# Recurrent layer: the head gates of steps 0 to 4 as three products of high and low parts, with low parts made on GpSimd

## The chip, the cores and the metric

The kernel runs on one core of a Trainium2 chip. The number that counts is the device time of one execution in microseconds, as the median of several executions. The chip's compute engines work side by side, each in its own program order, and wait for one another by semaphores: PE (TensorE, matrix products), DVE (VectorE), ACT (ScalarE), POOL (GpSimd) and SP (which here only starts transfers).

## The reference

A network of four layers on 256 positions of 1024 channels, in fp32: gated linear attention with a convolutional feed-forward part, softmax attention with another, then a recurrent layer ("LRU") and a short-convolution layer. Only the recurrent layer is touched:

```
u = h @ w_in;  gate, xb = split(u)                      # 1536 channels each
xc = causal_depthwise_conv(xb, conv_w, conv_b)          # 4 taps
g = sigmoid(einsum('bshi,hio->bsho', xc in 12 heads, gate_w) + gate_b)   # 12 heads of 128 -> 256
r, i = split(g);  log_a = -8 * r * softplus(-lambda)
h_t = exp(log_a) * h_{t-1} + sqrt(-expm1(2 log_a)) * i * xc
out = (h * silu(gate)) @ w_out
```

The head gates are the einsum: one 128x256 weight block for each of the 12 heads.

## The kernel before

All weights of the large products arrive by a stream of 1 MB units. Each unit is taken apart into two fp32r tensors (a 32-bit type whose products cost PE less than fp32 ones): ACT copies it to `w_hi` (L511) and DVE subtracts that from the raw unit to give `w_lo` (L1004). With activations in high and low parts too, a product is then three fp32r products, high x high, high x low and low x high (`PARTS`). The head gates are the exception in this layer: `gatew`, all 12 heads, is loaded whole by four transfers from POOL's queue (L492), and the gates multiply it with `xc` in plain fp32 (L2243).

The recurrent layer runs in six steps of two heads (`LRU_ITERS`), j = 0 to 5, written out on every engine as a loop in Python, so that the order on each engine is the order of the code. In step j:

- PE does `wide` for the unit "x" of step j (48 products, L1847, into one PSUM bank), `gates(j-1)`, `wide` for the unit "g" of step j (48 more, which waits for `gate_free` j), and from step 2 `lru_down(j-2)`, 24 products of 512 columns (L1862) that wait for `a_lo` of that step. In step 5, `gates(5)` stands between "g" and `lru_down(3)`.
- ACT takes the branch out of PSUM (`branch_taken`, xb), then the tanhs of `gates(j-1)` (L832: rg, ig) and `tanhs` (L854: ug), starts the convolution (`lru_taps`, L864: xc), and does `decays`, `roots` (L878, which wait for POOL's `clamped`), weight copies (L511), `gated` (L890) and `act_high` (L896: a_hi, which waits for DVE's `act_ready`).
- DVE does `inputs_gated(j-1)` (L1542: iu from ig and xc), six instructions of `lru_conv(j)` (L1555), after whose last `conv_ready` is raised, `recurrence(j-1)` (L1573, L1581, two scans L1566, L1587), weight subtractions (L1004), `lru_gate(j)` (L1601, which raises `gate_free`) and `act_low` (L1607: a_lo).
- POOL has one instruction in a step: it clamps ug at zero (L496).

`lru_taps` of step j waits for `inputs_gated(j-1)`, since that still reads the old xc; the convolution waits for the taps; and `gates(j)` on PE waits for the convolution.

## Time and profile before

| | us |
|---|---|
| median of 3 runs | 858.86 (858.73 to 859.99) |
| the profiled execution | 860.18 |
| its span, first to last instruction | 858.3 |
| busy PE | 847.7 |
| busy DVE | 677.3 |
| busy ACT | 542.2 |
| busy POOL | 38.3 |

The mean granted clock of TensorE is 0.999 of full speed. The busy times are sums over the whole program; the recurrent layer takes the stretch from about 570 to 680 us. One step of it from step 2 on takes 18.7 us.

### The profile page before, as it was taken

The numbers are of one execution on the slowest core, as the hardware profiler recorded it, in microseconds if no ns is written. First come the engines' busy times: TensorE is split into PE (matmuls) and PEld (weight loads), VectorE is DVE, ScalarE is ACT, GpSimd is POOL, SyncE is SP. The second block draws the span as 40 slices with busy tenths as digits, with TensorE's granted clock in tenths as the row PEclk, the third lists the DMA queues.
The fourth block names the chain that finished last, engine by engine and source line by source line (L and its number), as shares of the span: only waits on it lengthen the run. The fifth ranks groups of instructions, "written<-read, shape, count | busy, mean of one in ns | idle before, by whom it ended". The sixth has DMA issues, their size and how long they took to land.

```text
span 858.3 us, 13362 instructions
## 1 busy us (share of the span) xinstructions
PE 847.7 (99%) x4881; PEld 746.4 (87%) x4881; DVE 677.3 (79%) x970; ACT 542.2 (63%) x746; POOL 38.3 (4%) x57
## 2 busy tenths in 40 slices
PE   8999999999999999999999999999999999999997
PEld 7988889888888888889888888889999898888886
DVE  6799878887878798868887886787987877776764
ACT  5745656657556566576666656578988764555533
POOL 1000100000000041000000000000010100000000
PEclk9999999999999999999999999999999999999999
DMA  7554354666654344224666655435364046545511
GB/s 261 221 191 155 145 195 153 239 229 209 215 211 160 144 183 160 99 99 150 243 218 243 228 201 210 150 133 211 137 239 165 0 149 246 211 178 221 220 50 49
DMA packets 22908, 152.80 MB, mean 178 GB/s; under 512 B 2608, under 2 KB 2736, under 8 KB 5712
## 3 DMA queue, kind: packets, MB, share of 16 engines
q1 hardware_dynamic: 22176, 149.45, 47.5%
q0 software_dynamic: 544, 2.49, 0.9%
q8 instruction: 29, 0.48, 0.2%
q10 hardware_dynamic: 144, 0.26, 0.1%
q14 instruction: 15, 0.12, 0.0%
HBM read 151.14 MB, written 1.05 MB: 177 GB/s over the span
## 4 chain that ended last, share of the span: by engine, by line
PE 97%; DMA 1%; ACT 1%; DVE 1%; SPq 0%; issue 0%; ACTq 0%
PE ring L1798 38%; PE acc L1862 31%; PE ring L1847 10%; PE ring L1809 4%; PE acc L2085 3%; PE ring L1828 2%; PE ring L1933 1%; PE ring L2067 1%; PE ring L2243 1%; PE acc L1756 1%; DMA raw<-in_stream_dram 1%; PE ring L2125 1%; PE ring L2145 0%; PE acc L1882 0%; PE ring L1970 0%; PE ring L2162 0%
## 5 line engine op out<-in xcount | busy, mean ns | idle before, releaser
L1004 DVE TENSOR_TENSOR w_lo<-raw,w_hi 128x2048 fp32r<-128x2048 f32 (+1 forms) x145 | 317.9, 2197 | 5.8 <-ACT w_hi L511 5.7
L511 ACT ACTIVATE w_hi<-raw 128x2048 fp32r<-128x2048 f32 (+1 forms) x146 | 266.9, 1840 | 52.4 <-DMA raw<-in_stream_dram 50.0
L1798 PE MATMUL ring<-hh,w_hi 128*128 128x512 f32 x944 | 223.9, 390 | 0.0
L1798 PEld LDWEIGHTS ring<-hh,w_hi 128*128 128x128 f32 x944 | 175.3, 188 | 35.1
L1798 PEld LDWEIGHTS ring<-hh,w_lo 128*128 128x128 f32 x944 | 117.4, 192 | 2.5
L1798 PE MATMUL ring<-hh,w_lo 128*128 128x256 f32 x944 | 118.3, 283 | 0.0
L1862 PE MATMUL acc<-w_hi,a_hi 128*128 128x512 f32 x264 | 103.6, 392 | 0.1
L1862 PE MATMUL acc<-w_lo,a_hi 128*128 128x512 f32 x264 | 102.9, 390 | 0.0
L1862 PE MATMUL acc<-w_hi,a_lo 128*128 128x512 f32 x264 | 102.8, 389 | 0.0
L1847 PE MATMUL ring<-hh,w_hi 128*128 128x256 f32 x480 | 87.8, 285 | 0.0
L1122 DVE TENSOR_TENSOR usum<-ring,usum 128x512 f32<-128x512 f32 x65 | 44.7, 688 | 54.2 <-ACT usum L516 54.2
L1330 DVE SCALAR_TENSOR_TENSOR cacc<-usum,par,cacc 128x255 f32<-128x255 f32 x168 | 73.8, 481 | 15.0 <-ACT cacc L669 9.8
L1862 PE MATMUL acc<-w_hi,hh 128*128 128x512 f32 x256 | 84.2, 399 | 0.2 <-DVE hh L1043 0.2
L1847 PEld LDWEIGHTS ring<-hh,w_hi 128*128 128x128 f32 x480 | 75.4, 192 | 0.5
L1847 PE MATMUL ring<-hh,w_lo 128*128 128x256 f32 x240 | 67.9, 283 | 0.0
L516 ACT ACTIVATE usum<-ring 128x512 f32<-128x512 f32 x65 | 38.2, 588 | 44.4 <-PE ring L1798 42.6
L1862 PEld LDWEIGHTS acc<-w_hi,a_hi 128*128 128x128 f32 x264 | 49.6, 188 | 11.6 <-issue 0.9
L1862 PEld LDWEIGHTS acc<-w_hi,a_lo 128*128 128x128 f32 x264 | 49.6, 188 | 10.4
L1862 PEld LDWEIGHTS acc<-w_lo,a_hi 128*128 128x128 f32 x264 | 49.6, 188 | 9.8
L1862 PEld LDWEIGHTS acc<-w_hi,hh 128*128 128x128 f32 x256 | 48.1, 188 | 10.5 <-issue 0.4
L1862 PE MATMUL acc<-w_lo,hh 128*128 128x512 f32 x128 | 49.9, 390 | 0.0
L669 ACT ACTIVATE cacc<-usum,par 128x256 f32<-128x256 f32 x84 | 45.5, 590 | 6.9 <-DVE usum L1122 6.9
(247 smaller groups left out, 961.1 us busy)
## 6 DMA issues: line engine op xcount, KB each, us to landing
raw<-in_stream_dram SPq DMA_DIRECT2D x134, 1024.0 KB, 4.8
raw<-in_stream_dram SPq DMA_DIRECT2D x12, 512.0 KB, 3.8
gatew<-in_gatew_dram POOLq DMA_DIRECT2D x4, 384.0 KB, 4.2
x<-in_x_dram SPq DMA_DIRECT2D x2, 512.0 KB, 3.6
out_dram<-xn SPq DMA_DIRECT2D x3, 256.0 KB, 2.6
row<-in_row_dram POOLq DMA_DIRECT2D x1, 640.0 KB, 6.1
gup_raw<-in_gup_dram SPq DMA_DIRECT2D x3, 128.0 KB, 11.6
par<-in_par_dram SPq DMA_DIRECT2D x1, 274.0 KB, 4.8
```

Of the source, the lines that this page charges most:

```text
L511: nc.scalar.activation(w_hi[:, u % RING, 0:n], raw[:, u % RAW, 0:n], ACT.Copy).then_inc(hi_split, 1)
L516: nc.scalar.activation(usum[:, k, :, :], ring[:, 2 * k:2 * k + 2, S:2 * S], ACT.Copy).then_inc(cross_ready, 1)
L669: last = nc.scalar.activation(cacc[:, k, half, :], ring[:, 2, half * S:(half + 1) * S] if alone else usum[:, k, half, :], ACT.Identity, sc ...
L1004: nc.vector.tensor_tensor(w_lo[:, u % RING, 0:n], raw[:, u % RAW, 0:n], w_hi[:, u % RING, 0:n].bitcast(f32), ALU.subtract).then_inc(lo_spl ...
L1122: nc.vector.tensor_tensor(usum[:, k, :, :], ring[:, 2 * k:2 * k + 2, 0:S], usum[:, k, :, :], ALU.add).then_inc(summed, 1)
L1330: last = nc.vector.scalar_tensor_tensor(out=cacc[:, k, half, out_at], in0=at, scalar=par[:, bass.ds(c, 1)], in1=cacc[:, k, half, out_at], ...
L1798: last = nc.tensor.matmul(into, w_parts[part][:, u % RING, lo:lo + P], moving(kc), start=(n, kc) == (0, 0), stop=(n, kc) == (1, KC - 1), s ...
L1809: last = nc.tensor.matmul(both, w_hi[:, (u + k) % RING, lo:lo + P], hh[:, kc, :, t * P:(t + 1) * P], start=first, stop=end, skip_group_che ...
L1828: nc.tensor.matmul(ring[:, 2 * k + f, 0:S], w_lo[:, (u + k) % RING, lo:lo + P], h_hi[:, kc, :], start=False, stop=False, skip_group_check= ...
L1847: last = nc.tensor.matmul(ring[:, b, f * S:(f + 1) * S], w_parts[a][:, slot, lo:lo + P], h_parts[c][:, kc, :], start=kc == 0 and n == 0, s ...
L1862: last = nc.tensor.matmul(acc[:, t, half * 512:(half + 1) * 512], lhs(a, kc, t), w_parts[c][:, slot, j * D + half * 512:j * D + (half + 1) ...
L2085: last = nc.tensor.matmul(acc[:, t, half * 512:(half + 1) * 512], of_h(a, kc, t), w_parts[c][:, (U_AQ + n) % RING, j * D + half * 512:j * ...
```

## The change

For steps 0 to 4 (`SPLIT_GATES`), the head gates use the same three fp32r products as everything else. Of the weights, ACT makes `gw_hi` for the two heads of a step (a copy of 128x512), and POOL makes `gw_lo` by a subtraction, into the place of `gatew`. Of the activations, in step 0 ACT makes `xc_hi` and DVE makes `xc_lo`; in steps 1 to 4 POOL makes both, with a copy and then a subtraction, after `conv_ready`. PE waits for `gw_split` and `xc_split` in place of `conv_ready`. `gates(5)` stays in fp32.

```
+SPLIT_GATES = range(LRU_ITERS - 1)
...
+        gw_hi = put("gw_hi", [P, 2, 2 * P], f32r, at=gup_at)
+        gw_lo = put("gw_lo", [P, LRU_HEADS, 2 * P], f32r, at=gatew_at)
+        xc_lo = put("xc_lo", [P, 2, S], f32r, at=gup_at + 16 * P)
+        xc_hi = put("xc_hi", [P, 2, S], f32r, at=stage_at + 4 * 14 * S)
...
@@ gpsimd
+            def gate_weights_low(e):
+
+                pool.wait_ge(gw_hi_ready, e + 1)
+                nc.gpsimd.tensor_tensor(gw_lo[:, 2 * e:2 * e + 2, :], gatew[:, 2 * e:2 * e + 2, :], gw_hi[:, :, :].bitcast(f32),
+                                        ALU.subtract).then_inc(gw_split, 1)
+
+            gate_weights_low(0)
             for e in range(LRU_ITERS):
                 pool.wait_ge(tanh_ready, 2 * e + 2)
                 nc.gpsimd.tensor_scalar(ug[:, :, :], ug[:, :, :], 0.0, None, ALU.max).then_inc(clamped, 1)
+                if e + 1 in SPLIT_GATES:
+                    gate_weights_low(e + 1)
+                    pool.wait_ge(conv_ready, e + 2)
+                    nc.gpsimd.tensor_copy(xc_hi[:, :, :], xc[:, :, :]).then_inc(xc_hi_ready, 1)
+                    pool.wait_ge(xc_hi_ready, e + 2)
+                    nc.gpsimd.tensor_tensor(xc_lo[:, :, :], xc[:, :, :], xc_hi[:, :, :].bitcast(f32), ALU.subtract).then_inc(xc_split, 1)
@@ scalar
+            def gate_weights_high(e):
+
+                if e == 0:
+                    act.wait_ge(gatew_loaded, 16 * 4)
+                nc.scalar.activation(gw_hi[:, :, :], gatew[:, 2 * e:2 * e + 2, :], ACT.Copy).then_inc(gw_hi_ready, 1)
...
                 if j:
                     gates(e)
                     tanhs(e)
+                    if j in SPLIT_GATES:
+                        gate_weights_high(j)
+                else:
+                    gate_weights_high(0)
                 lru_taps(j)
                 if j < 2:
                     gated(j)
+                if j == 0:
+                    act.wait_ge(conv_ready, 1)
+                    nc.scalar.activation(xc_hi[:, :, :], xc[:, :, :], ACT.Copy).then_inc(xc_hi_ready, 1)
@@ vector
                 if j < 2:
                     lru_gate(j)
+                if j == 0:
+                    dve.wait_ge(xc_hi_ready, 1)
+                    nc.vector.tensor_tensor(xc_lo[:, :, :], xc[:, :, :], xc_hi[:, :, :].bitcast(f32), ALU.subtract).then_inc(xc_split, 1)
@@ tensor, gates(e)
-                pe.wait_ge(conv_ready, e + 1)
+                if e in SPLIT_GATES:
+                    pe.wait_ge(gw_split, e + 1)
+                    pe.wait_ge(xc_split, e + 1)
+                else:
+                    pe.wait_ge(conv_ready, e + 1)
...
-                        last = nc.tensor.matmul(ring[:, HEAD_BANKS[k], r * S:(r + 1) * S],
-                                                gatew[:, 2 * e + k, r * P:(r + 1) * P], xc[:, k, :],
-                                                start=True, stop=True, skip_group_check=True)
+                        into, at = ring[:, HEAD_BANKS[k], r * S:(r + 1) * S], slice(r * P, (r + 1) * P)
+                        if e not in SPLIT_GATES:
+                            last = nc.tensor.matmul(into, gatew[:, 2 * e + k, at], xc[:, k, :], start=True, stop=True, skip_group_check=True)
+                            continue
+                        for n, (a, c) in enumerate(PARTS):
+                            last = nc.tensor.matmul(into, (gw_hi[:, k, at], gw_lo[:, 2 * e + k, at])[a], (xc_hi, xc_lo)[c][:, k, :],
+                                                    start=n == 0, stop=n == 2, skip_group_check=True)
```

How the order of instructions stands on the engines, at three places. Lines are those of each kernel's own file, and the number behind a name is its buffer's. First POOL, from the last statistics of the layer before to those of the next; the kernel before:

```order
L492 DMA gatew_79<-in_gatew_dram 128x768 [waits used] x4
L448 TENSOR_SCALAR half_mean_64<-stat_66 128x1 [waits sumsq] x2
L496 TENSOR_SCALAR ug_120<-ug_120 128x512 [waits tanh_ready] x6
L448 TENSOR_SCALAR half_mean_64<-stat_66 128x1 [waits sumsq] x4
L186 UNCONDITIONAL_BRANCH
```

The changed kernel, for steps 0 to 2:

```order
L506 TENSOR_TENSOR gw_lo_128<-gatew_79,gw_hi_127 128x512 [waits gw_hi_ready]
L512 TENSOR_SCALAR ug_120<-ug_120 128x512 [waits tanh_ready]
L506 TENSOR_TENSOR gw_lo_128<-gatew_79,gw_hi_127 128x512 [waits gw_hi_ready]
L516 CAST xc_hi_130<-xc_117 128x512 [waits conv_ready]
L518 TENSOR_TENSOR xc_lo_129<-xc_117,xc_hi_130 128x512 [waits xc_hi_ready]
L512 TENSOR_SCALAR ug_120<-ug_120 128x512 [waits tanh_ready]
```

Between two clamps now stand three instructions of 128x512, four times over; the six clamps ran one after another with nothing between them.

Next PE at `gates(1)`, between the last products of "x" and the first of "g". Before:

```order
L1847 MATMUL ring<-hh_53,w_lo_51 128x256
L2243 MATMUL ring<-xc_117,gatew_79 128x256 [waits ri_ready,conv_ready]
L2243 MATMUL ring<-xc_117,gatew_79 128x256 x3
L1847 MATMUL ring<-hh_53,w_hi_50 128x256 [waits gate_free,lo_split]
L1847 MATMUL ring<-hh_53,w_hi_50 128x256
```

After, its first product and the start of the second:

```order
L1886 MATMUL ring<-hh_53,w_lo_51 128x256
L2291 MATMUL ring<-xc_hi_130,gw_hi_127 128x256 [waits ri_ready,xc_split,gw_split]
L2291 MATMUL ring<-xc_lo_129,gw_hi_127 128x256
L2291 MATMUL ring<-xc_hi_130,gw_lo_128 128x256
L2291 MATMUL ring<-xc_hi_130,gw_hi_127 128x256
```

Four fp32 products have become four triples, and the wait on the convolution one on the two low parts.

Last ACT, at the end of step 0 and into step 1. Before:

```order
L890 ACTIVATE sgate_124<-gg_122 128x512 [waits gate_summed]
L511 ACTIVATE w_hi_50<-raw_49 128x2048 [waits used,raw_loaded1]
L511 ACTIVATE w_hi_50<-raw_49 128x2048 [waits used,raw_loaded2]
L511 ACTIVATE w_hi_50<-raw_49 128x2048 [waits used,raw_loaded0]
L821 ACTIVATE xb_123<-ring 128x512 [waits conv_ready,used]
```

After:

```order
L919 ACTIVATE sgate_124<-gg_122 128x512 [waits gate_summed]
L942 ACTIVATE xc_hi_130<-xc_117 128x512 [waits conv_ready]
L533 ACTIVATE w_hi_50<-raw_49 128x2048 [waits used,raw_loaded1]
L533 ACTIVATE w_hi_50<-raw_49 128x2048 [waits used,raw_loaded2]
L533 ACTIVATE w_hi_50<-raw_49 128x2048 [waits used,raw_loaded0]
```

The copy of xc stands ahead of the three weight copies, and DVE's subtraction (xc_lo) likewise ahead of its three.

## Rows read from the trace of the kernel before

**Rows 1.** The page: busy us by engine; shares of the chain that ended last.
```profile
PE 847.7 (99%) x4881; PEld 746.4 (87%) x4881; DVE 677.3 (79%) x970; ACT 542.2 (63%) x746; POOL 38.3 (4%) x57
...
PE 97%; DMA 1%; ACT 1%; DVE 1%; SPq 0%; issue 0%; ACTq 0%
```
**Rows 2.** The chain in order of time, recurrent layer: start us, us, what, count.
```profile
601.54 1.73 PE ring L2243 x8
603.27 5.75 PE ring L1847 x48
...
666.98 9.57 PE acc L1862 x42
```
**Rows 3.** PE's timeline: start us, us, instruction, count; gates(1), lru_down(0), gates(2), gates(5).
```profile
601.38 1.89 PE L2243 MATMUL ring<-xc,gatew 128*128 128x256 f32 x8
...
608.86 0.40 PE L1862 MATMUL acc<-w_hi,a_hi 128*128 128x512 f32 x1
...
620.08 1.89 PE L2243 MATMUL ring<-xc,gatew 128*128 128x256 f32 x8
...
664.98 1.99 PE L2243 MATMUL ring<-xc,gatew 128*128 128x256 f32 x8
```
**Rows 4.** ACT's timeline in the recurrent layer: start us, us, instruction, count.
```profile
585.83 5.50 ACT L511 ACTIVATE w_hi<-raw 128x2048 fp32r<-128x2048 f32 x3
...
593.14 1.10 ACT L854 ACTIVATE ug<-rg,sp 128x256 f32<-128x256 f32 x2
...
603.53 0.62 ACT L896 ACTIVATE a_hi<-iu 128x512 fp32r<-128x512 f32 x1
```
**Rows 5.** POOL's timeline over the program; in brackets the idle time before.
```profile
2.01 0.41 POOL L430 TENSOR_SCALAR_AFFINE_SELECT causal<-causal 128x256 f32<-128x256 f32 x1
...
312.45 2.12 POOL L477 TENSOR_TENSOR tabs<-rope,row 128x256 f32<-128x256 f32 x1 [5.06 <-PE acc L1756]
314.54 0.46 POOL L478 TENSOR_TENSOR tabs<-rope,row 128x128 f32<-128x128 f32 x1
...
315.39 0.74 POOL L477 TENSOR_TENSOR tabs<-rope,row 128x256 f32<-128x256 f32 x1
316.10 2.51 POOL L478 TENSOR_TENSOR tabs<-rope,row 128x128 f32<-128x128 f32 x1
...
594.32 1.51 POOL L496 TENSOR_SCALAR ug<-ug 128x512 f32<-128x512 f32 x1 [25.06 <-ACT ug L854]
```
**Rows 6.** DVE's timeline beside POOL's instructions of 312 to 318 us.
```profile
311.68 2.29 DVE L1004 TENSOR_TENSOR w_lo<-raw,w_hi 128x2048 fp32r<-128x2048 f32 x1 [0.73 <-ACT w_hi L511]
...
318.21 2.55 DVE L1004 TENSOR_TENSOR w_lo<-raw,w_hi 128x2048 fp32r<-128x2048 f32 x1
```
**Rows 7.** DVE's timeline in the recurrent layer; in brackets the idle time before, its ender.
```profile
594.37 1.11 DVE L1542 SCALAR_TENSOR_TENSOR iu<-ig,xc 128x512 f32<-128x512 f32 x1
596.64 2.71 DVE L1555 SCALAR_TENSOR_TENSOR xc<-xb,par,xc 128x255 f32<-128x255 f32 x6 [1.16 <-ACT xc L864]
...
600.58 0.69 DVE L1581 TENSOR_TENSOR iu<-su,iu 128x512 f32<-128x512 f32 x1
...
607.63 0.68 DVE L1607 TENSOR_TENSOR a_lo<-iu,a_hi 128x512 fp32r<-128x512 f32 x1
608.45 0.69 DVE L1542 SCALAR_TENSOR_TENSOR iu<-ig,xc 128x512 f32<-128x512 f32 x1
...
618.49 0.68 DVE L1601 SCALAR_TENSOR_TENSOR gg<-sgate,ring 128x512 f32<-128x512 f32 x1
...
641.57 0.69 DVE L1542 SCALAR_TENSOR_TENSOR iu<-ig,xc 128x512 f32<-128x512 f32 x1 [1.34 <-ACT ig L832]
...
660.26 0.69 DVE L1542 SCALAR_TENSOR_TENSOR iu<-ig,xc 128x512 f32<-128x512 f32 x1 [2.86 <-ACT ig L832]
662.22 2.71 DVE L1555 SCALAR_TENSOR_TENSOR xc<-xb,par,xc 128x255 f32<-128x255 f32 x6 [1.27 <-ACT xc L864]
```
**Rows 8.** Busy us (instructions) of one step: PE, PEld, DVE, ACT, POOL; clock, DMA.
```profile
633.00:651.70 18.70, 18.70 (x129) 17.53 (x128) 15.91 (x18) 16.48 (x20) 1.49 (x1) 1.00 0.44 169
```

More of the change, by code:

```diff
@@ L208, in two_block_kernel @@
         wr = put("wr", [P, KC, 2 * GLA_RANK])
+        gup_at = top
         gup = put("gup", [RANKS, 2, GLA_KEYS], f32r)
@@ L267, in two_block_kernel @@
         yy, actl = ig, iu
+        gw_hi = put("gw_hi", [P, 2, 2 * P], f32r, at=gup_at)
+        gw_lo = put("gw_lo", [P, LRU_HEADS, 2 * P], f32r, at=gatew_at)
+        xc_lo = put("xc_lo", [P, 2, S], f32r, at=gup_at + 16 * P)
+        xc_hi = put("xc_hi", [P, 2, S], f32r, at=stage_at + 4 * 14 * S)
+        assert stage_at + 4 * 16 * S <= gatew_at
         pp, ct, sgs, ys, acts = stage(stage_at, gatew_at, *((n, [P, S]) for n in ("pp", "ct", "sgs", "ys", "acts")))
@@ L323, in two_block_kernel @@
         ri_ready, tanh_ready, decay_ready, sqrt_ready = (sem(n) for n in ("ri_ready", "tanh_ready", "decay_ready", "sqrt_ready"))
+        gw_hi_ready, gw_split, xc_hi_ready, xc_split = (sem(n) for n in ("gw_hi_ready", "gw_split", "xc_hi_ready", "xc_split"))
         cross_ready, summed = sem("cross_ready"), sem("summed")
```

## The prediction, made before the changed kernel ran

> **What bounds the kernel now.** I read the page first: PE is busy 847.7 of 858.3 us and makes up 97% of the chain that ended last [rows 1]. So time comes off only where PE's own work shrinks, and whatever makes PE wait is added in full unless it waits there already. The chain in order of time shows the recurrent layer as an unbroken run of PE pieces [rows 2]: eight records of the head gates take 1.73 us, the 48 products of a streamed unit 5.75 us. Then comes the question that decides this case: how close behind PE the other engines are. One step of 18.70 us has 15.91 us of DVE and 16.48 us of ACT in it, and 1.49 us of POOL [rows 8]. DVE's timeline tells where its spare time lies [rows 7]: an iu that waits for the gates' tanh 1.34 us in step 4 (641.57) and 2.86 us in step 5 (660.26). The 1.16 to 1.27 us ahead of each convolution are no spare time, since ACT's taps wait for iu itself. And at one place DVE is exactly on PE's heels: the last convolution ends at 662.22 + 2.71 = 664.93, and gates(5) starts at 664.98 [rows 7, 3].
>
> **What is removed.** A step's head gates are four fp32 products in 1.73 us. Three fp32r products of 256 columns go at 5.75 / 48 = 0.12 us each, so four triples take 12 x 0.12 = 1.44 us [rows 2]. Saving 0.29 us a step, 1.45 us over steps 0 to 4. The bounds are 0, if the first product after a change of type costs what the old ones did, and 1.45; I take 1.45, as the rows have the same shape. It is less than 0.2% of the time (1.72 us, about what a measurement of this kernel can tell from no change).
>
> **What POOL's new instructions take.** Subtractions of 128x512 with two SBUF operands are not in the trace. Undisturbed, 128x256 took 0.74 us and 128x128 0.46 us (314.54) [rows 5]: 0.28 us more for 128 more columns, so 0.74 + 2 x 0.28 = 1.30 us. Right after being held up they are shorter: the first L477 ended at 314.57, 0.60 us after the DVE subtraction beside it ended (313.97), and a 128x128 one ended 0.34 us after one (318.61 against 318.27) [rows 5, 6]. By that, 0.60 + 2 x 0.26 = 1.12 us. The copy of 128x512 lies between 0.65 us (0.41 for the select of 128x256, doubled less a start) and 1.49 us (the clamp, same shape) [rows 5, 8]. I take 0.8, nearer to the select, since a copy computes nothing, and keep both ends.
>
> **What they do to DVE.** This is the main term. The first L477 stretched to 2.12 us beside a DVE subtraction, and L478 to 2.51 us [rows 5, 6]: a POOL instruction that reads SBUF waits for the end of a DVE instruction with two SBUF operands, and slips in between two of them. It goes the other way too: beside the clamp begun at 594.32, the iu of 594.37 took 1.11 us and not 0.69, 0.42 us more; the weight subtraction behind L478 took 2.55 and not 2.29, 0.26 us more [rows 5, 6, 7]. The first holds DVE for one operand of 512, the second for two of 128. For two of 512 that is 2 x 0.42 = 0.84 by the one and 4 x 0.26 = 1.04 by the other; I take 0.95 us for a subtraction and 0.40 for a copy. DVE's instructions around them (convolution, recurrence, weight subtractions, a_lo) nearly all have two SBUF operands.
>
> The Trainium skill has a sharper form of this ("SBUF — State Buffer", § Who interferes with whom): whoever issues first gets the shared pair for the whole instruction and the other fully blocks. The clamp row speaks against the whole instruction (0.42 us of 1.51), the L478 row hardly does; what it would make of the sum is a rival below.
>
> **The sum, on DVE.** How late DVE runs against before, step by step:
> - Step 0: ACT's copy of xc (0.62 us, by a_hi's row [rows 4]) stands ahead of three weight copies that run back to back (585.83, 5.50 us), and DVE's subtractions follow those: 0.6 us late. DVE's own xc_lo fits in its wait for the first copy, and gates(0) has 3.5 us from the first convolution. The gw_hi copies of steps 0 to 3 lie in ACT's waits for xb or iu: free. In step 4 it costs ACT 0.62 us, which waits later for DVE anyway.
> - Step 1: the clamp ends some 2.1 us after ACT's ug began its second half (594.24 to 595.83); gw_lo follows and overlaps the convolution's start (596.64 before) by 0.4. xc_lo falls in the recurrence: 0.95. Late by 1.95.
> - Steps 2 and 3: gw_lo 0.9, xc_hi 0.4, xc_lo 0.95, so 2.25 each; late by 6.45. Then the wait of 1.34 us at 641.57 is used up (5.1), and the clamp, which met an idle DVE before, now holds it 0.42 (5.5).
> - Step 4: gw_lo 0.5 (it falls partly into the gap ahead of the convolution), 0.4 and 0.95; late by 7.4. The 2.86 us at 660.26 are used up (4.5), and a clamp of 0.42 again: 4.9 us late at the last iu, and so at the last convolution.
> That convolution had no slack [rows 3, 7]: gates(5) starts 4.9 us later than before, whatever PE saved ahead of it. From there 42 products ran at PE's own pace [rows 2]; those, DVE's chain and ACT's all shift alike, and nothing gives it back.
>
> **The sum, on PE.** It must be less than that to be hidden. In step 1, gates(1) are due at 601.38 - 0.29 = 601.09 [rows 3]. The convolution ends at 599.35 + 0.6 + 0.4 = 600.3; the copy runs to 601.2, the subtraction waits for DVE's iu to end (601.5) and ends at 602.6. PE waits 1.6 us, with a copy of 1.49 us 2.3; I take 1.9. At lru_down(0) PE is then at 608.86 - 0.58 + 1.9 = 610.2, and a_lo, which ended at 608.31, ends at 608.31 + 1.95 = 610.3 [rows 3, 7]: no more than 0.1 on top. In step 2, `gate_free` comes at 619.17 + 4.2 = 623.4 and PE wants it at 620.08 + 1.73 + 1.4 - 0.29 = 622.9: 0.5 more. In steps 3 and 4 xc_lo is there over 3 us ahead (7 and 11 us of slack before). So PE reaches gates(5) about 1.9 + 0.1 + 0.5 - 1.45 = 1.1 us late, waits there until 4.9, and the latter is the result.
>
> **The forecast.** 860.18 + 4.9 = 865.1 us for the profiled execution, whose time lay 1.3 us above the median of the runs; against the median, 858.86 + 4.9 = 863.8 us. The same case with its cheap ends (0.85 for a subtraction, 0 for the copy, 0.4 for gw_lo) gives +2.0, with its dear ends (1.1, 0.42, each meets DVE) +6.5: 860.9 to 865.4 us.
>
> **Rivals.**
> - **PE's wait in step 1 only.** If half of DVE's blocks don't occur (POOL slips into DVE's semaphore gaps, or its reads are buffered), the idle 4.20 us swallow the rest. Then the time is PE's: +1.9 - 1.45 = +0.5, and up to +1.5 with the slow copy: 859.4 us. For it: the split at 315.98 was not stretched although L477 was still running. Against: two stretched instructions in the trace. 0.22.
> - **A gain.** The two low parts come by the time PE gets there in step 1. That needs copy and subtraction in 1.2 us together after 599.9, less than the subtraction alone by its rows. Then 858.86 - 1.45 = 857.4 us: the whole saving, still within 0.2%. 0.04. It decides for itself from a `xc_split` before 601.1.
> - **Whole-instruction locks.** The blocks are the durations: 1.2 for a subtraction, 1.1 for a copy. 0.6 + 1.6 + 3.5 + 3.5 + 0.42 + 2.9 + 0.42 - 4.20 = +8.7, so 867.6 us. The clamp row is against it, as said. 0.08. This is what the page of the skill named above would give.
> - **Something heavier between** (fp32r output slower on POOL than fp32, both new waits colliding with weight subtractions of 2.29 us so that xc_lo is late in steps 2 to 4 as well): 865.5 to 868 us. 0.08.
> The forecast itself has 0.58.
>
> **Chances and range.** Slower by over 0.2% (above 860.6) are the forecast, the two heavy cases, and little of the first rival: 0.73. Within 0.2% is the first rival with the gain, since that is at most 1.45 us: 0.24. Faster by over 0.2% would need more than PE has to give: 0.03. The range goes from 859.2, which takes in most of the first rival, to 867.0.
>
> **What the profile after would show.** Head gates: 12 records with 1.44 us in the chain for steps 0 to 4. POOL: subtractions of 1.1 to 1.3 us when undisturbed, up to 2.3 us more beside weight subtractions. PE: one wait of about 2 us before gates(1), on POOL; one of about 4 us before gates(5), on DVE's xc. DVE: iu, su and the first instruction of a convolution stretched by 0.4 to 1 us, and no idle time left before the iu of steps 4 and 5. If the last iu still has idle time ahead of it, DVE's blocks were over-priced and the first rival holds. If the wait at gates(1) is missing, POOL's prices are wrong.

## The result, and the profile after

The changed kernel takes 862.95 us (median of 6 runs, 862.35 to 864.80), the kernel before beside it 858.88 us (6 runs, 858.68 to 859.99). The ratio is 1.0048, with a 95% interval of 1.0038 to 1.0058: 4.1 us slower, where 4.9 were forecast. The profiled execution took 864.03 us, with a span of 862.3 and a granted clock of 0.999.

The page of the changed kernel, busy us by engine and the shares of the chain that ended last, to be held against [rows 1]:

```profile
PE 847.8 (98%) x4901; PEld 746.3 (87%) x4901; DVE 684.8 (79%) x971; ACT 545.3 (63%) x752; POOL 58.4 (7%) x70
...
PE 83%; DVE 9%; issue 4%; ACT 2%; DMA 1%; POOL 0%; ACTq 0%; DVEq 0%; SPq 0%; POOLq 0%
```

PE has as much work as before, but the chain no longer runs through it alone: 9% is DVE's. Where DVE took it over, the waits of PE in the recurrent layer tell (us in total, times, longest), and the chain in order of time:

```profile
PE ring L2288 <- DVE xc L1591: 2.2, 1, 2.2
PE ring L2291 <- issue: 1.4, 1, 1.4
```

```profile
662.01 1.11 DVE iu L1578
...
664.27 0.89 DVE xc L1591 x2
...
665.19 0.89 DVE xc L1591 x2
...
667.03 1.99 PE ring L2288 x8
669.03 9.53 PE acc L1901 x42
```

L2291 is gates(1). The view names no releaser for its wait ("issue"), but its first product starts at 601.67, right behind POOL's xc_lo (599.94 + 1.62 = 601.56): it waits for the low parts. L2288 is gates(5), which waits 2.2 us for the last convolution. DVE's timeline of the changed kernel (start us, us, instruction, idle before) shows how it got late. Its recurrent layer begins 0.95 us earlier than that of the kernel before (first convolution at 581.00, against 581.95), so 0.95 has to be added to compare a start with [rows 7]:

```profile
596.23 2.96 DVE L1591 SCALAR_TENSOR_TENSOR xc<-xb,par,xc 128x255 f32<-128x255 f32 x6 [1.16 <-ACT xc L893]
...
599.70 0.71 DVE L1609 SCALAR_TENSOR_TENSOR iu<-aa,iu 128x512 f32<-128x512 f32 x1
600.44 1.67 DVE L1617 TENSOR_TENSOR iu<-su,iu 128x512 f32<-128x512 f32 x1
...
609.29 1.11 DVE L1578 SCALAR_TENSOR_TENSOR iu<-ig,xc 128x512 f32<-128x512 f32 x1
611.57 2.94 DVE L1591 SCALAR_TENSOR_TENSOR xc<-xb,par,xc 128x255 f32<-128x255 f32 x6 [1.17 <-ACT xc L893]
...
615.14 0.98 DVE L1617 TENSOR_TENSOR iu<-su,iu 128x512 f32<-128x512 f32 x1
616.15 2.27 DVE L1602 TENSOR_TENSOR_SCAN ig<-aa,iu 128x256 f32<-128x256 f32 x2
...
624.67 2.28 DVE L1040 TENSOR_TENSOR w_lo<-raw,w_hi 128x2048 fp32r<-128x2048 f32 x1
...
644.44 1.10 DVE L1578 SCALAR_TENSOR_TENSOR iu<-ig,xc 128x512 f32<-128x512 f32 x1
...
662.01 1.10 DVE L1578 SCALAR_TENSOR_TENSOR iu<-ig,xc 128x512 f32<-128x512 f32 x1
664.27 2.71 DVE L1591 SCALAR_TENSOR_TENSOR xc<-xb,par,xc 128x255 f32<-128x255 f32 x6 [1.17 <-ACT xc L893]
```

and POOL's beside it:

```profile
599.94 1.62 POOL L518 TENSOR_TENSOR xc_lo<-xc,xc_hi 128x512 fp32r<-128x512 f32 x1
609.25 1.49 POOL L512 TENSOR_SCALAR ug<-ug 128x512 f32<-128x512 f32 x1 [7.68 <-ACT ug L883]
610.72 1.28 POOL L506 TENSOR_TENSOR gw_lo<-gatew,gw_hi 128x512 fp32r<-128x512 f32 x1
614.57 1.00 POOL L516 CAST xc_hi<-xc 128x512 fp32r<-128x512 f32 x1 [2.57 <-DVE xc L1591]
615.66 1.64 POOL L518 TENSOR_TENSOR xc_lo<-xc,xc_hi 128x512 fp32r<-128x512 f32 x1
625.31 2.99 POOL L512 TENSOR_SCALAR ug<-ug 128x512 f32<-128x512 f32 x1 [8.02 <-ACT ug L883]
```

Read the two together, row by row, for step 2. The clamp lies on iu (1.11 for 0.69, +0.42), the end of gw_lo on the first instructions of the convolution (2.94 for 2.70, +0.24), the copy on iu<-su (0.98 for 0.69, +0.29), xc_lo on the scans (2.27 for 1.27, +1.0; in step 1 on iu<-su, 1.67 for 0.69). That makes 1.95 us. The idle time before the iu of steps 4 and 5 (641.57 and 660.26 in [rows 7]) is gone: 644.44 and 662.01 carry no bracket.

A convenient measure is the time from the start of the first convolution of the layer to the end of the last, the one that gates(5) wait for. Before it is 662.22 + 2.71 - 581.95 = 82.98 us [rows 7] (581.95 is the start of the first one in the same timeline), after it 664.27 + 2.71 - 581.00 = 85.98: **3.0 us more**. The remaining 1.1 us of the 4.1 come behind it; they are looked for below. The table gives this measure, read from the one trace of each kernel, beside the difference of the medians to the kernel before in the same comparison.

| kernel | lateness by the trace, us | median, us | less before's median, us | ratio (95%) |
|---|---|---|---|---|
| changed kernel | +3.0 | 862.95 | +4.1 | 1.0048 (1.0038 to 1.0058) |
| the same again | +3.0 | 863.68 | +4.5 | 1.0047 (1.0035 to 1.0060) |
| fp32 products, all splitting | +3.0 | 861.98 | +2.8 | 1.0035 (1.0022 to 1.0048) |
| low parts by memset | -0.7 | 858.41 | -0.8 | 0.9992 (0.9983 to 1.0001) |
| without step 1 | +3.0 | 864.02 | +4.8 | 1.0052 (1.0039 to 1.0065) |
| steps 0 to 2 | +1.3 | 860.25 | +1.3 | 1.0017 (1.0008 to 1.0026) |
| xc parts by ACT and DVE | -0.9 | 858.23 | -1.0 | 0.9995 (0.9987 to 1.0004) |
| GpSimd: weights' low parts alone | -0.5 | 858.33 | -0.6 | 0.9995 (0.9986 to 1.0004) |
| GpSimd: xc parts alone | +2.1 | 860.69 | +1.8 | 1.0024 (1.0015 to 1.0033) |
| changed, PE's wait filled | +3.0 | 862.75 | +2.8 | 1.0034 (1.0021 to 1.0048) |
| without step 1, wait filled | +3.0 | 862.05 | +2.1 | 1.0036 (1.0022 to 1.0049) |
| without step 1, again | +3.0 | 864.31 | +4.4 | 1.0055 (1.0041 to 1.0069) |
| low parts by DVE | -1.2 | 857.47 | -1.4 | 0.9983 (0.9974 to 0.9992) |

### The profile page after: what moved, and what is told of

Read it like the earlier page. It is cut to its first block, busy times and chain, and to the rows that moved or that the text cites. A ratio compares the mean times of both kernels' runs of the same rounds, so it can differ in the third digit from the quotient of the medians.

```text
span 862.3 us, 13422 instructions
## 1 busy us (share of the span) xinstructions
PE 847.8 (98%) x4901; PEld 746.3 (87%) x4901; DVE 684.8 (79%) x971; ACT 545.3 (63%) x752; POOL 58.4 (7%) x70
## 4 chain that ended last, share of the span: by engine, by line
PE 83%; DVE 9%; issue 4%; ACT 2%; DMA 1%; POOL 0%; ACTq 0%; DVEq 0%; SPq 0%; POOLq 0%
PE ring L1837 36%; PE acc L1901 28%; PE ring L1886 3%; DVE w_lo L1040 3%; PE acc L2124 3%; PE ring L1848 2%; DVE xc L1591 2%; DMA raw<-in_stream_dram 1%; PE ring L1972 1%; PE ring L2106 1%; PE acc L1795 1%; PE ring L1867 1%; PE ring L2164 1%; PE ring L1951 1%; ACT xc L893 1%
```

## The experiments

Two theories stood against each other. **D**: POOL's reads hold DVE up, and DVE's lateness comes out at gates(5). **P**: it is PE's own wait before gates(1), behind a slow xc_lo.

**All the splitting, but fp32 products.** POOL, ACT and DVE do what they do in the changed kernel; PE waits for the convolution alone and multiplies in fp32 as before. Since `gatew` and xc must now stay until they are read, gw_lo gets another place and ACT two waits more (for `gw_split` ahead of gw_hi, for `xc_split` ahead of the taps); they don't show in DVE's rows.

```
@@ gates(e)
-                if e in SPLIT_GATES:
-                    pe.wait_ge(gw_split, e + 1)
-                    pe.wait_ge(xc_split, e + 1)
-                else:
-                    pe.wait_ge(conv_ready, e + 1)
+                pe.wait_ge(conv_ready, e + 1)
...
+                        last = nc.tensor.matmul(into, gatew[:, 2 * e + k, at], xc[:, k, :], start=True, stop=True, skip_group_check=True)
```

> All the added work on ACT, DVE and POOL stays (gw_hi, gw_lo, xc_hi, xc_lo), but PE multiplies in fp32 as before and waits for the convolution alone; the low parts go unused, and the old xc is kept until POOL has read it. Theory D (POOL's reads make DVE late, and that lateness comes out at gates(5)): DVE does what it does in the changed kernel, so gates(5) start 3.0 us late again, with no wait at gates(1): 862.2 to 863.0 us. Theory P (the cost is PE's wait for POOL at gates(1), 1.4 us, and what follows from it): no such wait is left, 858.9 to 859.5 us.

Measured 861.98 us, +2.8. PE has no new wait before gates(1) and saves nothing, and the loss is there all the same; gates(5) wait for xc:

```profile
PE ring L2287 <- DVE xc L1595: 1.5, 1, 1.5
PE acc L1905 <- DVE a_lo L1647: 1.1, 1, 1.1
```

The last convolution is 3.0 us late, to the hundredth as in the changed kernel. P falls: with no wait before gates(1) and no cheaper products, the same lateness comes out at the end.

**Low parts by memset.** POOL's subtractions of steps 1 to 4 are replaced by memsets of the same size that read nothing; clamps and copies stay.

```
+                if e:
+                    nc.gpsimd.memset(idle_low[:, :, :], 0.0).then_inc(gw_split, 1)
+                    return
...
-                    nc.gpsimd.tensor_tensor(xc_lo[:, :, :], xc[:, :, :], xc_hi[:, :, :].bitcast(f32), ALU.subtract).then_inc(xc_split, 1)
+                    nc.gpsimd.memset(idle_low[:, :, :], 0.0).then_inc(xc_split, 1)
```

> The changed kernel with POOL's subtractions of steps 1 to 4 replaced by a memset of the same 128x512 into an unused place: POOL writes and reads nothing there. The low parts of step 0 are used in all five steps, so the gates of steps 1 to 4 leave out their own low parts. Copy and order stay. Theory D: DVE's stretches of 1.0 us (xc_lo) and 0.25 us (gw_lo) are gone, what is left (0.5 from step 0, 0.3 a copy) vanishes in the 4.2 us of idle time; xc_split of step 1 comes about 0.3 us after PE; 5 x 0.29 saved, so 857.6 to 858.2 us. If the mere presence of more instructions and waits on POOL cost the time: 861.5 to 863 us. Theory P: 1.1 us of the wait goes, 861.8 us.

Measured 858.41 us, 0.2 above the range that D gave and 0.8 us under the kernel before; the interval of the ratio (0.9983 to 1.0001) just holds 1. DVE in step 3 of this kernel, and the last iu:

```profile
625.67 2.70 DVE L1596 SCALAR_TENSOR_TENSOR xc<-xb,par,xc 128x255 f32<-128x255 f32 x6 [1.16 <-ACT xc L898]
...
629.01 0.98 DVE L1622 TENSOR_TENSOR iu<-su,iu 128x512 f32<-128x512 f32 x1
630.03 1.27 DVE L1607 TENSOR_TENSOR_SCAN ig<-aa,iu 128x256 f32<-128x256 f32 x2
...
658.02 0.69 DVE L1583 SCALAR_TENSOR_TENSOR iu<-ig,xc 128x512 f32<-128x512 f32 x1 [1.76 <-ACT ig L866]
```

Convolution and scans have their old lengths, the copy alone still costs 0.29, and 1.76 us of idle are left before the last iu. So it is the subtractions that stretch DVE. A memset also ends sooner (0.52 us), so this run by itself doesn't tell a read from a long stay on the engine. The clamp speaks for the read: it stays 1.49 us and reads one operand, and costs DVE 0.42; a subtraction of 1.30 us reads two and costs 1.0. No run took a long instruction that reads nothing.

**Without step 1.** The split in steps 0, 2, 3 and 4 (`SPLIT_GATES = [0, 2, 3, 4]`, the waits counted accordingly); all else as changed.

> The changed kernel with step 1 left in fp32, so that POOL adds nothing there. Theory D: DVE is less late by 0.25 + 0.98 = 1.2 us only, gates(5) start 1.8 us late instead of 3.0: 861.5 to 861.9 us, though PE has no wait before gates(5) any more. Theory P: with the wait at gates(1) gone, four steps save 1.2 us: 857.7 us.

Measured 864.02 us, +4.8, and both numbers were missed. PE no longer waits before gates(1), as meant, yet the last convolution is again 3.0 us late. DVE and then POOL in step 2 and at the start of step 3:

```profile
610.39 3.74 DVE L1592 SCALAR_TENSOR_TENSOR xc<-xb,par,xc 128x255 f32<-128x255 f32 x6 [1.16 <-ACT xc L894]
...
624.30 2.71 DVE L1041 TENSOR_TENSOR w_lo<-raw,w_hi 128x2048 fp32r<-128x2048 f32 x1
626.94 1.78 DVE L1579 SCALAR_TENSOR_TENSOR iu<-ig,xc 128x512 f32<-128x512 f32 x1
```

```profile
610.56 1.47 POOL L507 TENSOR_TENSOR gw_lo<-gatew,gw_hi 128x512 fp32r<-128x512 f32 x1
...
624.25 1.49 POOL L513 TENSOR_SCALAR ug<-ug 128x512 f32<-128x512 f32 x1 [7.33 <-ACT ug L884]
625.72 2.45 POOL L507 TENSOR_TENSOR gw_lo<-gatew,gw_hi 128x512 fp32r<-128x512 f32 x1
```

The step left out should have given 1.25 us back, but gw_lo of step 2 now begins with the convolution instead of ending with its start, and costs it 1.03 us (3.74 for 2.71) instead of 0.24; the next one falls on iu, 1.78 for 0.69. By step 4 DVE was as late as in the changed kernel. A block's price hangs on what it meets, and one taken away shifts the others. Why the same 3.0 us make +4.8 here is the subject of the last experiments.

**Steps 0 to 2 alone** (`SPLIT_GATES = [0, 1, 2]`).

> The split gates in steps 0 to 2 alone, the rest as in the changed kernel. Theory D (POOL's reads make DVE late, and what DVE's own waits do not take up comes out at gates(5)): by the DVE rows of the changed kernel the lateness is 0.53 us in step 0, 1.25 in step 1 and 1.94 in step 2, 3.7 in all; the waits of 1.34 and 2.86 us before the iu of steps 4 and 5 take it up whole, so gates(5) is not late by it. What is left is PE's account: 1.4 us of wait before gates(1) and 0.3 on a_lo, less 3 x 0.29 saved, +0.8: 859.5 to 859.9 us. Rival, that lateness once made stays on DVE to the end: +2.4 and more, 861.3 us.

Measured 860.25 us, +1.3, above the 0.6 to 1.0 expected but far from the rival's 2.4. The lateness was swallowed: there is idle time again before the last iu.

```profile
660.01 0.69 DVE L1579 SCALAR_TENSOR_TENSOR iu<-ig,xc 128x512 f32<-128x512 f32 x1 [1.97 <-ACT ig L862]
```

From 608.60 on the chain, as far as the last gates, is PE's alone. What PE lost is more than its wait at gates(1): a_lo of step 0 ends at 608.54, 1.8 us late by this kernel's start (608.31 before, less 1.55), since it stands behind the stretched step 1 on DVE, and lru_down(0) wait for it. That is the second way in which DVE's lateness reaches PE, hidden in the changed kernel by gates(5).

**POOL makes the weights' low parts alone; POOL makes the xc parts alone.** In the first, copy and subtraction of xc leave POOL; in the second, the work on weights after step 0 leaves ACT and POOL. PE's products take the parts of step 0 for what is not made.

```
@@ weights alone
-                    pool.wait_ge(conv_ready, e + 2)
-                    nc.gpsimd.tensor_copy(xc_hi[:, :, :], xc[:, :, :]).then_inc(xc_hi_ready, 1)
-                    pool.wait_ge(xc_hi_ready, e + 2)
-                    nc.gpsimd.tensor_tensor(xc_lo[:, :, :], xc[:, :, :], xc_hi[:, :, :].bitcast(f32), ALU.subtract).then_inc(xc_split, 1)
...
@@ xc alone
-                    gate_weights_low(e + 1)
...
-                    if j in SPLIT_GATES:
-                        gate_weights_high(j)
...
```

> GpSimd makes the low parts of the weights in all steps; it makes nothing of xc in steps 1 to 4, where the products take the parts of step 0 (so the values are not the reference's) and wait for the convolution. Theory D: a gw_lo costs DVE 0.24 us by the rows of the changed kernel, 1.0 at worst where it meets the convolution in full, so DVE's lateness is 0.53 + 4 x 0.24 + 0.42 = 1.9 us, at worst 4.0, below the 4.20 us of its own waits. Nothing reaches gates(5), PE waits nowhere, and the whole saving of 1.45 us shows: 857.4 us. Rival, locks for the whole instruction (1.3 us a subtraction): 0.53 + 5.2 + 0.42 - 4.2 = +2.0, 860.9 us. Rival, that ACT's weight copies or the products themselves carry the loss: 861 us or more.

> GpSimd makes both parts of xc in steps 1 to 4; the parts of the weights are those of step 0 throughout (so the values are not the reference's), and neither ACT nor GpSimd works on weights after step 0. Theory D: per step 0.98 us for xc_lo and 0.29 for the copy from step 2 on, so 0.53 + 0.98 + 1.29 + 0.42 + 1.29 - 1.34 + 1.29 - 2.86 + 0.42 = +2.0 us at gates(5): 860.9 us (860.4 to 861.2). PE's wait of 1.4 us before gates(1) stays but is hidden by it. Rival, that the wait at gates(1) alone counts: 1.4 - 1.45 = 0, 858.8 us. Rival, that gw_lo is the dear one: below 859.

Measured 858.33 us (-0.6) and 860.69 us (+1.8). The second is within 0.2 us of the sum, and its trace has iu<-su at 0.98 and the scans at 2.27 in each step from step 2, with convolutions of 2.70 and 2.71. So POOL's work on xc is the dear part: alone it makes 2.1 of the 3.0 us, and xc_lo is most of it (1.0 us a step, the copy 0.29). The first kept DVE's lateness under its idle time, as forecast, but its median is 0.9 us above the forecast 857.4 and shows only 0.6 of the 1.45 us of saving, with an interval that holds 1: in its trace PE waited 0.7 us once for a_lo, the same way as above. Here too gw_lo met the convolution in full in one step:

```profile
642.58 3.81 DVE L1587 SCALAR_TENSOR_TENSOR xc<-xb,par,xc 128x255 f32<-128x255 f32 x6 [1.36 <-ACT xc L889]
```

```profile
642.59 1.30 POOL L506 TENSOR_TENSOR gw_lo<-gatew,gw_hi 128x512 fp32r<-128x512 f32 x1
```

**The xc parts by ACT and DVE.** Steps 0, 2, 3 and 4; from step 2 on ACT copies xc after its roots and DVE subtracts after its recurrence; POOL keeps gw_lo, and makes both parts of xc in step 0.

```
+                if j and j in SPLIT_GATES:
+                    act.wait_ge(conv_ready, j + 1)
+                    nc.scalar.activation(xc_hi[:, :, :], xc[:, :, :], ACT.Copy).then_inc(xc_hi_ready, 1)
...
+                if j and j in SPLIT_GATES:
+                    dve.wait_ge(xc_hi_ready, NTH_SPLIT[j] + 1)
+                    nc.vector.tensor_tensor(xc_lo[:, :, :], xc[:, :, :], xc_hi[:, :, :].bitcast(f32), ALU.subtract).then_inc(xc_split, 1)
...
```

> Steps 0, 2, 3 and 4 split, step 1 in fp32. POOL makes xc_hi and xc_lo in step 0 only, where DVE waits for ACT anyway; in steps 2 to 4 ACT makes xc_hi after its roots and DVE makes xc_lo after the recurrence; gw_lo stays on POOL. Theory D: DVE is late by 0.6 + 0.25 a step and 0.4 for a clamp, 3.4 us in all at most, less than its 4.2 us of idle time: PE never waits, 4 x 0.29 saved, 857.5 to 858.0 us. Theory P says the same, so this run tests that the products' saving can be had at all. If DVE's own subtraction costs as much as POOL's: 859 to 861 us.

Measured 858.23 us, 0.2 above the range, 1.0 us under the kernel before in the median; the interval of the ratio (0.9987 to 1.0004) just holds 1. DVE's idle time is just used up: none is left before the last iu, and PE waits 0.2 us for the last convolution, where D had no wait. DVE now does 0.69 us more work itself in a step and is less late than when it was held up for 1.0 to 1.3 us.

**Both low parts by DVE.** The same, and from step 2 on gw_lo too is DVE's, in its wait for ACT's taps; POOL still makes gw_lo and both xc parts of step 0.

```
@@ vector
+                if j and j in SPLIT_GATES:
+                    dve.wait_ge(gw_hi_ready, NTH_SPLIT[j] + 1)
+                    nc.vector.tensor_tensor(gw_lo[:, 2 * j:2 * j + 2, :], gatew[:, 2 * j:2 * j + 2, :], gw_hi[:, :, :].bitcast(f32), ALU.subtract).then_inc(gw_split, 1)
@@ gpsimd
-                if e + 1 in SPLIT_GATES:
-                    gate_weights_low(e + 1)
...
```

> A version that should beat both: split gates in steps 0, 2, 3 and 4; from step 2 on DVE makes gw_lo in its wait for ACT's taps (1.16 to 1.27 us, the subtraction takes 0.69) and xc_lo after the recurrence (0.69), ACT makes both high parts; GpSimd only clamps. Theory D: DVE is late by 0.53 + 0.42 + 3 x 0.69 = 3.0 us at most, less 4.20 of waits, so nothing is late, and 4 x 0.29 = 1.16 us are gained: 857.7 us. It should lie 0 to 0.5 us below the version in which GpSimd still made gw_lo (858.2). Rival, that DVE's new waits for ACT's copies (0.62 us each) push the taps later in each step: +0.6 a step on DVE, still under its waits, so the same; only if both come on top of each other does it end above 858.9.

Measured 857.47 us, 0.2 under the forecast; the ratio is 0.9983 (0.9974 to 0.9992), so this version beats the kernel before, by 1.4 us, and the changed one, by 5.5 (between comparisons; each ratio is against the same kernel before). Its DVE in step 4 and at the last iu, and its chain:

```profile
641.11 0.91 DVE L1651 TENSOR_TENSOR gw_lo<-gatew,gw_hi 128x512 fp32r<-128x512 f32 x1
642.17 2.71 DVE L1590 SCALAR_TENSOR_TENSOR xc<-xb,par,xc 128x255 f32<-128x255 f32 x6 [0.15 <-ACT xc L892]
...
648.15 0.69 DVE L1659 TENSOR_TENSOR xc_lo<-xc,xc_hi 128x512 fp32r<-128x512 f32 x1
...
658.01 0.69 DVE L1577 SCALAR_TENSOR_TENSOR iu<-ig,xc 128x512 f32<-128x512 f32 x1 [1.37 <-ACT ig L860]
```

```profile
655.66 1.42 PE ring L2293 x12
657.08 5.75 PE ring L1888 x48
662.83 1.89 PE ring L2290 x8
664.72 9.54 PE acc L1903 x42
```

The wait ahead of the convolution has shrunk from 1.27 to 0.15 us, with gw_lo in it; 1.37 us are still free before the last iu, and PE runs through without a wait from step 0 to step 5. What is gained is what the prediction priced: four times 1.73 less 1.42, 1.2 us.

**The changed kernel again**, for the 1.1 us behind the last convolution. In its first trace the loss of 3.0 us there had become 4.9 by the end (862.3 - 666.98 = 195.3 us, against 858.3 - 664.93 = 193.4 before). ACT's rows at the start of the short-convolution layer, of the kernel before, then of the changed one:

```profile
700.77 1.92 ACT L511 ACTIVATE w_hi<-raw 128x2048 fp32r<-128x2048 f32 x1 [2.48 <-DMA raw<-in_stream_dram]
```

```profile
704.78 1.92 ACT L533 ACTIVATE w_hi<-raw 128x2048 fp32r<-128x2048 f32 x1 [4.48 <-DMA raw<-in_stream_dram]
```

> The changed kernel again, without an edit. Its median was 4.1 us above the kernel before, while its trace showed gates(5) only 3.0 us later; in that trace, whose execution lay 1.1 us above the median, the short-convolution layer lost another 1.9 us, ahead of it a transfer of raw weights that ACT waited 4.48 us for (2.48 before). The version with all the splitting work but fp32 products had the same 3.0 us on DVE and came out at +2.8. If the late transfer belongs to some executions alone, more executions give a lowest time near 861.9 and a median between that and 862.9, and a trace without it ends 193.4 us after the last convolution. If it belongs to the changed kernel, the median is 862.9 again, and the trace shows the wait of over 4 us once more.

Measured 863.68 us (861.11 to 864.82, 6 runs), +4.5. The profiled execution, of 862.69 us, has the 3.0 us again and a wait of 3.60 us for the transfer. Neither expectation fits: the median is above both, the wait lies between. One execution, 861.11 us, is even below 858.9 + 3.0, and no trace shows why.

**Is it TensorE's clock?** The trace of the version without step 1 had shown another thing: gates(5) took 3.47 us in its chain and not 1.99. Three kernels were compared on that: the changed one and that version, each with PE's wait at gates(5) filled by products whose result gates(5) overwrite (14 and 22 of them), and that version once more as it was.

```
@@ gates(e)
+                if e == LRU_ITERS - 1:
+                    pe.wait_ge(ri_ready, 2 * e)
+                    for n in range(14):
+                        nc.tensor.matmul(ring[:, HEAD_BANKS[0], 0:S], gw_hi[:, 0, 0:P], xc_hi[:, 0, :], start=True, stop=True, skip_group_check=True)
```

> The changed kernel, and while PE waits for the last convolution it does 14 products of 128x256 (1.7 us by 0.12 us each) into the bank that gates(5) overwrite. DVE is as late as before, 3.0 us. Theory C: part of what the changed kernel loses beyond those 3.0 us is TensorE's clock, which in one trace fell to half for 3.5 us after PE had waited 3.0 us at this place. With the wait filled the clock can't fall there: no execution with a clock below 0.998, a median of 862.0 to 862.4 us, narrow like that of the version with fp32 products (861.8 to 862.7). Rival, the late transfer in the next layer alone: filling changes nothing, 862.9 to 863.7 us, and the wait of ACT for it is 3.6 us or more.

> The version without step 1, with 22 such products (2.6 us) in PE's wait of 3.0 us. Theory C: 1.7 us (1.5 in the gates, 0.2 behind them) go where the clock had fallen: gates(5) take 1.9 us and not 3.47, the granted clock stays at 1.00 in that stretch, the median falls from 864.0 to 862.3 us. Rival, the transfer alone: 864 us again.

> The version without step 1 once more, beside the one with the filled wait. Theory C: 864.0 us again, gates(5) at half the clock for some 3.5 us after a wait of 3.0 us. If this trace has the same wait and no fall of the clock, the fall belongs to some executions only.

The kernel before took 859.94 us beside these three, about 1 us more than beside the others, so they are held against each other. Without step 1: 864.31 us as it was, 862.05 filled. Windows behind the wait (window, us, then busy us and instructions of PE, PEld, DVE, ACT and POOL, the granted clock, DMA share and GB/s) and the chain's piece for gates(5), first as it was:

```profile
667.50:669.00 1.50, 1.50 (x5) 1.23 (x4) 1.47 (x3) 1.49 (x3) 0.00 (x0) 0.50 0.00 0
669.00:670.00 1.00, 1.00 (x4) 0.73 (x4) 0.93 (x3) 0.04 (x1) 0.00 (x0) 0.50 0.00 0
```

```profile
666.61 3.57 PE ring L2289 x8
```

and then filled:

```profile
667.50:669.00 1.50, 1.50 (x9) 1.29 (x8) 1.47 (x3) 1.49 (x4) 0.00 (x0) 1.00 0.00 0
669.00:670.00 1.00, 1.00 (x6) 0.82 (x5) 0.97 (x2) 0.47 (x2) 0.00 (x0) 1.00 0.00 0
```

```profile
666.70 1.99 PE ring L2293 x8
```

After PE's wait of 3.0 us the granted clock was 0.50 (1.2 GHz in place of 2.4), and the same eight records took 3.57 us in place of 1.99; with products in the wait it stayed at 1.00. So in that version a fall of the clock costs some 1.7 us behind the wait, in both its traces (1.5 to 1.6 in gates(5), the rest in the products after them), and the profiled execution with the wait filled is 1.6 us shorter (863.61 and 862.05). The medians of the two differ by 2.3 us, of five executions each; the intervals of their ratios, 1.0041 to 1.0069 and 1.0022 to 1.0049, still overlap a little.

For the changed kernel the answer is weaker. Its wait is 2.2 us, and neither of its traces has a fall. Filled, it takes 862.75 us (862.14 to 863.07), narrow as forecast, but 0.35 us above C's range for the median and 0.15 under the rival's, and ACT's wait for the transfer is 3.10 us, where the rival had 3.6 or more; by the ratios, 1.0034 against 1.0048 and 1.0047, it lost less, but the intervals overlap. Of the 12 executions unfilled, 861.11 to 864.82 us, four show a mean clock of 0.996 or 0.997, at 862.90, 863.89, 864.80 and 864.82 us; of the five filled none is below 0.998. A fall in some executions fits that, but one of the four is not slow, and no trace of this kernel has a fall: for the changed kernel the clock is not shown.

**The rest: one transfer.** It is the 1 MB of raw weights that ACT waits for in its two rows above (2.48 us before, 4.48 in the changed kernel). It is issued 29.9 us after the last convolution in every trace read for it, that of the kernel before included (31.6 where the clock had fallen), and in nine of them the chain passes through it. How long it took, and the time from the last convolution to the end of the span:

| trace | transfer, us | to the end, us |
|---|---|---|
| fp32 products | 6.00 | 193.4 |
| without step 1, again (clock fell, 1.7) | 6.11 | 195.4 |
| without step 1, wait filled | 6.21 | 193.7 |
| low parts by memset | 6.81 | 194.2 |
| changed, wait filled | 6.92 | 194.4 |
| xc parts alone | 6.96 | 194.4 |
| changed, again | 7.02 | 194.4 |
| without step 1 (clock fell, 1.7) | 7.78 | 197.0 |
| changed | 7.91 | 195.3 |

193.4 us, plus what the transfer takes over 6.0, plus the clock's loss, gives each of them within 0.2 us. In the kernel before it took 5.9 us (193.4 to the end), and in the other four versions 5.1 to 5.8 (193.1 to 193.4): below 6.0 it costs nothing. That is a reading of traces, and no run changed the transfer by itself. It changes from execution to execution, 7.91 and 7.02 us in the two traces of the changed kernel; of xc parts alone, 7 of 11 runs lie between 860.63 and 860.80 us and the profiled one, with 6.96 us, at 861.71, which fits. Where the last convolution was 2.1 us late or more it took 6.0 to 7.9 us (eight traces), where it was not 5.1 to 6.8 (six). What sets it, and whether a late DVE makes it longer, stays open.

## Why the prediction was right, and where not

- **What bounds, and where it comes out: right.** DVE's lateness at the last convolution sets the end, and PE's saving is not seen. The run with fp32 products shows it directly.
- **The saving: right.** The triple products take 1.42 us, for 1.44 forecast: from 587.19 to 588.61 in step 0 of the changed kernel, whose chain doesn't pass through them, and in the chain of the version with the low parts by DVE.
- **POOL's durations: right for the subtraction** (1.28 to 1.30 us undisturbed, forecast 1.30). The shorter 1.12 us after a hold-up came too: xc_lo ended 1.15 us after the DVE instruction beside it in step 1 (601.56, against 599.70 + 0.71 = 600.41) and 1.18 us after it in step 2 (617.30, against 615.14 + 0.98 = 616.12). The copy takes 0.61 alone and 1.00 beside DVE; 0.8 was taken.
- **A block of 0.95 us by a subtraction: right for xc_lo** (0.98 to 1.0), and it is most of the loss. The copy was 0.40 and is 0.29.
- **gw_lo: the term that was mis-sized.** The sum had 0.9 us in steps 2 and 3 and 0.5 in step 4, 2.3 in all; measured 0.24 each, 0.7. For step 1 it had read the overlap off the rows (0.4; 0.25 came); for steps 2 and 3 it took nearly the full price, and no row stands behind that. The price of a full meeting was not at fault (1.03 and 1.10 us where it began with the convolution in two of the experiments), but the place: in the changed kernel gw_lo runs in DVE's gap of 1.16 to 1.17 us ahead of the convolution and only its last 0.43 us meets it (610.72 + 1.28 = 612.00, against 611.57). The gap ahead of a convolution is no spare time for lateness, as the prediction says, but work that ends inside it is free: the first 0.85 us of gw_lo here, and DVE's own gw_lo in the version with both low parts by DVE.
- **The clamp: one more than forecast.** It falls on iu in step 2 as well (609.29, 1.11 us), +0.42. Later clamps begin inside a weight subtraction (625.31, in that of 624.67), stretch to 2.99 us, and iu has 1.10 us all the same.
- **The sum for DVE: 4.9 forecast, 3.0 measured.** The waits of 1.34 and 2.86 us were used up as said; three times 0.1 for the copy, the 1.6 of gw_lo, and 0.42 the other way for the clamp make 1.5 of the difference of 1.9.
- **PE's waits.** Before gates(1) 1.4 us, forecast 1.9 (1.6 with the copy of 0.8 us, 2.3 with the slow one): the copy was short, and DVE 0.2 us less late there (0.53 + 0.25, for 0.6 + 0.4). On a_lo at lru_down(0) 0.3, forecast 0.1. On `gate_free` 0.5 was forecast, about 0.1 seen. PE came 0.8 us late to gates(5) (667.03 + 0.95 - 2.2 = 665.8, against 664.98 [rows 3]), forecast 1.1, and waited 2.2 us there, not 4.
- **The ends of the range.** Added again with the terms that it names, the cheap case gives +2.2 and not +2.0, and the dear one, with gw_lo in full in every step, +7.3 and not +6.5. The result lies between them either way. The 2.1 us from ug's second half to the clamp's end run from 593.69 (half of the 1.10 us from 593.14) to 595.83; the 594.24 beside them is ug's end.
- **The total: in part luck.** The 863.8 us came within 0.9 us of the 862.95, but not by the right sum: of +4.1, the mechanism forecast carries 3.0, and 1.1 come from what no step had. In the trace that is a transfer in the next layer, which took 7.9 us where 6.0 would have cost nothing and is by then on the chain; how the median's 1.1 us divide is not shown. By its own mechanism alone the kernel would take 861.9 us, which the range held.
- **The rivals.** "PE's wait in step 1 only" fell with the fp32 products (+2.8 without that wait). "Whole-instruction locks" had 1.2 us for a subtraction and 1.1 for a copy. For the subtraction that is not far off: xc_lo's 1.62 to 1.64 us hold its own wait for DVE, and of the 1.15 and 1.18 us that it had left behind it, DVE's next instructions grew by 0.98 and 1.0. It fails for the copy, which had 0.43 us left when iu<-su began (614.57 + 1.00, against 615.14) and held it for 0.29, and for the clamp, which had 1.45 us left when iu began at 609.29 and held it for 0.42; and it took every gw_lo in full. The Trainium skill ("SBUF — State Buffer", § Who interferes with whom) says that whoever issues first has the shared pair for the whole instruction and the other fully blocks. By these rows that nearly holds for POOL's subtractions and not for its copy and clamp, which read one operand.

## What to carry to other kernels

Work given to an idle POOL is not free when it reads SBUF beside DVE instructions with two operands there: price it on DVE's queue, 1.0 us for a subtraction of 128x512 here, where DVE itself would have done it in 0.69, and rather put it into a gap that DVE already has. Sum lateness only up to the next real idle time; what is left at the first place without slack is the result. A block taken away shifts the others, so its neighbours' prices (0.24 or 1.03 us for the same gw_lo) must be read again.

## What the runs showed of the hardware that was not expected

- What one POOL instruction of 128x512 adds to DVE's instructions beside it is nearly the same in every step and run, where these read two operands from SBUF: a tensor_tensor 0.98 to 1.10 us on a full meeting, a copy 0.29, a tensor_scalar on one operand 0.42. POOL pays too: xc_lo 1.64 for 1.30, the copy 1.00 for 0.61. In step 1 the copy (599.25 to 599.86) met DVE's gg<-sgate,ring, one operand of which comes from PSUM: it kept its 0.61 us and gg its 0.68.
- Which of the two pays depends on which began first. Begun 0.64 us inside a weight subtraction of 128x2048, the clamp took 2.99 us and the subtraction its 2.28; begun 0.05 us ahead of one (without step 1, 624.25 and 624.30), the clamp took 1.49 and the subtraction 2.71.
- From 626.87 to 644.44 and on to 662.01 a step of the changed kernel takes 17.57 us, with no idle time before iu: DVE sets the pace. PE's own step took 18.70 [rows 8]. So even with POOL beside it a late DVE catches up with PE by 1.1 us in a step, and blocks in early steps cost less at the end than they add up to.
- A wait of PE of 3.0 us was followed by half the clock for some 3.5 us, in two traces; waits of 2.1 and 2.2 us were not, in two. Such a wait cost 1.7 us more behind itself, over half as much again.
- The same 1 MB transfer, issued at the same place, took 5.1 to 7.9 us to land over 14 traces.
